# Down-projection of a decoder layer: one weight sum kept in DRAM, other bank order, other order of the last rows

## The reference

```python
D_MODEL = 2048; SEQ = 512; D_FF = 5632; EPS = 1e-6

def rms_norm(x, g):
    return x * lax.rsqrt(jnp.mean(x * x, axis=-1, keepdims=True) + EPS) * g

def conv_glu_ffn(h, w_up, conv_w, conv_b, w_down):
    u = h @ w_up
    c = causal_depthwise_conv_width_3(u, conv_w) + conv_b
    gate, val = jnp.split(c, 2, axis=-1)
    return (jax.nn.gelu(gate, approximate=True) * val) @ w_down   # (512, 5632) @ (5632, 2048)

x = x + rms_norm(y, g_mix_post)            # attention part, unchanged here
f = conv_glu_ffn(rms_norm(x, g_ffn_pre), w_up, conv_w, conv_b, w_down)
x = x + rms_norm(f, g_ffn_post)
```

## Time and profile before

| | us |
|---|---|
| time before, median of 3 runs | 2064.43 (2063.61 to 2065.13) |
| the profiled execution, its own time | 2064.49 |
| its span, from the first to the last instruction | 2062.7 |
| PE busy | 1998.8 (97%) |
| DVE busy | 1545.6 (75%) |
| ACT busy | 1012.3 (49%) |
| mean granted TensorE clock | 0.993 of full speed |

### The profile page before, as it was taken

One profiled execution on the slowest core, in us unless ns is written; L12 is line 12 of the kernel. 1 busy time (PEld: TensorE's weight loads), 2 busy tenths in 40 slices (PEclk: granted clock), 3 DMA queues, 4 the chain that ended last, 5 costly groups with the idle time before them and its releaser, 6 DMA issues.

```text
span 2062.7 us, 31761 instructions
## 1 busy us (share of the span) xinstructions
PE 1998.8 (97%) x12510; PEld 1796.4 (87%) x12510; DVE 1545.6 (75%) x2028; ACT 1012.3 (49%) x1549; POOL 0.7 (0%) x6
## 2 busy tenths in 40 slices
PE   8999999999999889999999999999999999999994
PEld 6888888888887789999999999999999787878773
DVE  5522543445446889898898889888998998899998
ACT  7422433435435655555555555545555554554442
POOL 0000000000000000000000000000000000000000
PEclk9999999999999999999999999999999999999998
DMA  8433232211636534324423432442344776668793
GB/s 317 138 123 118 77 93 82 82 62 62 244 124 211 177 103 160 119 100 151 149 101 121 163 117 100 136 163 101 111 145 154 237 245 211 224 214 295 254 361 125
DMA packets 218895, 323.26 MB, mean 157 GB/s; under 512 B 9134, under 2 KB 140622, under 8 KB 216444
## 3 DMA queue, kind: packets, MB, share of 16 engines
q1 hardware_dynamic: 218076, 315.99, 45.0%
q10 hardware_dynamic: 672, 5.24, 0.6%
HBM read 292.60 MB, written 32.54 MB: 158 GB/s over the span
## 4 chain that ended last, share of the span: by engine, by line
PE 83%; DVE 10%; issue 3%; ACT 3%; DMA 1%; DVEq 0%; SPq 0%; ACTq 0%
PE ring L2034 11%; PE ring L2036 11%; PE ring L2035 11%; PE ring L2295 9%; PE ring L2297 9%; PE ring L2296 9%; PE side L2295 4%; PE side L2297 4%; PE side L2296 4%; PE side L2034 2%; PE side L2035 2%; PE side L2036 2%; DVE w_lo L1721 2%; DVE raw L1730 1%; PE side L2110 1%
## 5 line engine op out<-in xcount | busy, mean ns | idle before, releaser
L1442 DVE TENSOR_TENSOR w_lo<-raw,w_hi 128x512 fp32r<-128x512 f32 x256 | 169.7, 688 | 275.2 <-ACT w_hi L1027 275.2
L1721 DVE TENSOR_TENSOR w_lo<-q,w_hi 128x1024 fp32r<-128x1024 f32 (+1 forms) x262 | 308.3, 1177 | 79.7 <-ACT w_hi L1244 69.5
L2295 PE MATMUL ring<-s_hi,w_hi 128*128 128x256 f32 x1008 | 286.8, 284 | 6.7 <-ACT snaps L1336 3.5
L2296 PE MATMUL ring<-s_lo,w_hi 128*128 128x256 f32 x1008 | 286.4, 284 | 0.0
L2297 PE MATMUL ring<-s_hi,w_lo 128*128 128x256 f32 x1008 | 286.4, 284 | 0.0
L1721 DVE TENSOR_TENSOR w_lo<-raw,w_hi 128x1024 fp32r<-128x1024 f32 x214 | 249.3, 1173 | 37.1 <-ACT w_hi L1244 26.9
L1027 ACT ACTIVATE w_hi<-raw 128x512 fp32r<-128x512 f32 x256 | 151.8, 624 | 187.7 <-PE ring L2036 171.1
L1244 ACT ACTIVATE w_hi<-q 128x1024 fp32r<-128x1024 f32 x174 | 183.6, 1056 | 97.5 <-PE side L2297 54.2
L2295 PEld LDWEIGHTS ring<-s_hi,w_hi 128*128 128x128 f32 x1008 | 194.8, 193 | 7.3 <-ACT snaps L1336 3.9
L2295 PE MATMUL ring<-a_hi,w_hi 128*128 128x256 f32 x688 | 195.3, 284 | 4.0 <-issue 3.3
L2034 PE MATMUL ring<-w_hi,act_hi 128*128 128x512 f32 x488 | 192.9, 395 | 3.3 <-DVE w_lo L1442 2.7
(11 more groups left out here) (298 smaller groups left out, 4672.8 us busy)
## 6 DMA issues: line engine op xcount, KB each, us to landing
q<-in_w_up SPq DMA_DIRECT2D x65, 1024.0 KB, 5.0
q<-in_w_down SPq DMA_DIRECT2D x66, 512.0 KB, 4.5
raw<-in_w_down SPq DMA_DIRECT2D x66, 512.0 KB, 4.5
raw<-in_w_in SPq DMA_DIRECT2D x28, 1024.0 KB, 5.4
raw<-in_w_out SPq DMA_DIRECT2D x24, 1024.0 KB, 4.9
raw<-in_w_up SPq DMA_DIRECT2D x23, 1024.0 KB, 6.9
q<-sa_d SPq DMA_DIRECT2D x22, 512.0 KB, 4.4
raw<-in_w_mem_kv SPq DMA_DIRECT2D x8, 1024.0 KB, 7.1
```

The costliest lines, as they stand in the source:

```text
L1442: dve.tensor_tensor(w_lo[:, s, q], raw[:, s, q], w_hi[:, s, q].bitcast(F32), ALU.subtract).then_inc(lo_done, 1)
L1721: dve.tensor_tensor(lo, src, hi.bitcast(F32), ALU.subtract).then_inc(hp_lo_done, 1)
L2295: pe.matmul(dst, hi, b_hi, start=first, stop=False, skip_group_check=True)
L2296: pe.matmul(dst, hi, b_lo, start=False, stop=False, skip_group_check=True)
```

## The change

- T3 is stored to DRAM in passes 0 and 1 (`spill_t3`, 44 stores of 256 KB to the new `t3_d`), each issued by SP one `w` after the DVE sum it stores. Passes 2 and 3 load it back in place of one weight block and make T2 from it with one addition; T1 is not made there. A step of these passes is loaded by three DMAs of 256 KB instead of two of 512 KB. The first four loads of pass 2 wait for stores that have just been issued.
- In passes 0 and 1 T3 and T1 are made by one 1024-column addition with a repeated operand instead of two of 512 columns.
- The products get other halves and banks (half 0: p3 in `bank_x`, p7 in `bank_y`; half 1: p1 in `bank_v`, p5 in `bank_w`). ACT copies three products per m out of PSUM instead of one (`keep` of "12", "21", "11"), and only p5's bank is freed by a DVE sum.
- At the end the order is half 0 for m = 0 and 1, then half 1 for m = 0 and 1; the rows are finished in the order 0, 1, 2, 3. The mean of the n = 0 half is prepared earlier on DVE (`mean0`) and added inside ACT's square root. The n = 0 half of rows 0 and 1 is finished by PE and ACT: two fp32 matmuls for each 512 columns (diagonal of rstd times f, identity times x1), then an ACT copy (`row_diagonal`, `row_out`).

```diff
-TAIL_T = (0, 2, 1, 3)
+TAIL_T = (0, 1, 2, 3)
@@ load_down(d), spill_t3(d), in the loop of SP
                 if v < 2:
-                    both(0, k1)
-                    sp.dma_start(seg(d, 2), w_down_d[k2, n2]).then_inc(down_in[s], 16)
+                    sp.dma_start(seg(d, 2, 2)..., w_down_d[k1, :]...[:, :, n1]).then_inc(down_in[s], 16)
+                    sp.dma_start(seg(d, 0), w_down_d[k2, n2]).then_inc(down_in[s], 16)
                 else:
-                    both(2, k1)
-                    both(0, k2)
+                    k = p if v == 2 else 2 * N_PAIRS - 1 - p
+                    sp.wait_ge(t3_out[k % 4], 16 * (k // 4 + 1))
+                    if 2 * N_PAIRS <= d < 2 * N_PAIRS + 4:
+                        sp.wait_ge(t3_out[s], 16 * ((d - 4) // 4 + 1))
+                    sp.dma_start(seg(d, 1), t3_d[v % 2, p]).then_inc(down_in[s], 16)
+                    sp.dma_start(seg(d, 3), w_down_d[k1, n1]).then_inc(down_in[s], 16)
+                    sp.dma_start(seg(d, 0), w_down_d[k2, n1]).then_inc(down_in[s], 16)
+            def spill_t3(d):
+                v, p = pass_pair(d)
+                sp.wait_ge(block_sum, block_sum_count(d, "T3"))
+                sp.dma_start(t3_d[v, p], seg(d, 1)).then_inc(t3_out[d % 4], 16)
...
                     sp.wait_ge(hp_lo_done, H_DOWN + e - 6)
                     load_down(e // 2)
+                e = w - H_DOWN + 4
+                if e >= 0 and e % 2 == 0 and e < 4 * N_PAIRS:
+                    spill_t3(e // 2)
...
-            for i, t in enumerate(TAIL_T):
-                for n in range(2):
-                    sp.wait_ge(out_ready, 2 * i + n + 1)
+            for n, t in ((1, 0), (1, 1), (0, 0), (1, 2), (0, 1), (0, 2), (1, 3), (0, 3)):
+                if n or t > 1:
+                    sp.wait_ge(out_ready, t + 1 if t < 2 else 2 * t - n)
+                else:
+                    sp.wait_ge(row_kept, 2 * t + 2)
@@ ACT
                 if w in (w_at(0), w_at(1)):
+                    for what in ("12", "21"):
+                        for m in range(2):
+                            keep(w == w_at(1), what, m)
+                if w in (w_at(0) + 1, w_at(1) + 1):
                     for m in range(2):
-                        keep(w == w_at(1), m)
+                        keep(w == w_at(1) + 1, "11", m)
...
+            f_square(1, 0)
+            row_root(0)
+            f_square(1, 1)
+            row_root(1)
+            row_diagonal(0)
+            row_diagonal(1)
+            for t in range(2, TT):
                 f_square(1, t)
-                take_root(NB_F + i, 1)
+                row_root(t)
+            row_out(0)
+            row_out(1)
@@ DVE
             def sums_a(d):
-                plus(d, 3, 1, 2)
-                dve.wait_ge(block_sum, block_sum_count(d, "T3"))
-                plus(d, 1, 1, 0)
+                if d >= 4:
+                    dve.wait_ge(t3_out[d % 4], 16 * (d // 4))
+                halves = raw_slots[d % 4].rearrange("p (b h n) -> p b h n", b=2, h=2)
+                b12 = seg(d, 3)
+                dve.tensor_tensor(halves[:, :, 1, :], halves[:, :, 0, :], both_times(b12), ALU.add)...
             def sums_b(d):
-                plus(d, 3, 3, 2)
-                dve.wait_ge(block_sum, block_sum_count(d, "T1"))
                 plus(d, 1, 1, 3)
...
-                if w == w_at(0) or w == w_at(1):
-                    sum_f(w == w_at(1), "12a", 0)
-                    sum_f(w == w_at(1), "12a", 1)
                 if w == w_at(0) + 1 or w == w_at(1) + 1:
-                    for m in range(2):
-                        sum_f(n, "22a", m)
-                        sum_f(n, "21a", m)
                     sum_f(n, "12b", 0)
                     sum_f(n, "12b", 1)
+                    for m in range(2):
+                        sum_f(n, "21a", m)
+                        sum_f(n, "22a", m)
+                    sum_f(n, "12c", 0)
+                    sum_f(n, "12c", 1)
...
+            for m in range(2):
+                dve.wait_ge(down_ready, m + 1)
+                for what in ("11", "12", "22", "21b"):
+                    sum_f(1, what, m)
+                times_gain(TT + m, 1, m)
+                if m == 1:
+                    for k in range(2):
+                        dve.wait_ge(down_ready, 3 + k)
+                        sum_f(1, "21", k)
+                finish(m, (1,))
+            for t in (2, 3):
+                times_gain(TT + t, 1, t)
+                finish(t)
@@ PE
-            for m in range(2):
-                for half, names in ((0, ("p6", "p2")), (1, ("p4",))):
+            for half, names in ((0, ("p6", "p2")), (1, ("p4",))):
+                for m in range(2):
...
+            pe.wait_ge(x1_back, 16 * TT)
+            for t in range(2):
+                pe.wait_ge(diag_ready, t + 1)
+                for h in range(2):
...
+                    pe.matmul(row_bank(t)[h][:, :], diagonal(t), f0[:, t, h, :], start=True, stop=False)
+                    pe.matmul(row_bank(t)[h][:, :], ident[:, :], x1_back_at[:, t, ...],
+                              start=False, stop=True).then_inc(row_added, 1)
```

More of the change, by code:

```diff
@@ L531, in build @@
         down_in = [sem(f"down_in{i}") for i in range(4)]
+        t3_out = [sem(f"t3_out{i}") for i in range(4)]
+        mean_ready, diag_ready, row_added, row_kept = (sem("mean_ready"), sem("diag_ready"), sem("row_added"),
+                                                       sem("row_kept"))
         x1_back, g_f_in = sem("x1_back"), sem("g_f_in")
@@ L670, in blocks_in @@
         def blocks_in(d):
-            return down_in[d % 4], sum(32 if True else 0 for k in range(d % 4, d + 1, 4))
+            return down_in[d % 4], sum(32 if k < 2 * N_PAIRS else 48 for k in range(d % 4, d + 1, 4))
         def block_sum_count(d, name):
             if d < 2 * N_PAIRS:
-                return 2 * d + ("T3", "T1").index(name) + 1
-            return 4 * N_PAIRS + 3 * (d - 2 * N_PAIRS) + ("T1", "T2", "T4").index(name) + 1
+                return d + 1
+            return 2 * N_PAIRS + 2 * (d - 2 * N_PAIRS) + ("T2", "T4").index(name) + 1
         def half_width(e):
@@ L740, in f_row, with diagonal, row_bank @@
             return (f0, f1)[n][:, t, :, :]
+        def diagonal(t):
+            return tokens[:, 3072 + t * P:3072 + (t + 1) * P]
+        def row_bank(t):
+            return (bank_x, bank_y)[t % 2]
         def w_at(v):
@@ L1266, in item_to_hi, with keep @@
                 act.activation(left_at(kind, slot)[0], stage_at(i), ACT.Copy).then_inc(a_hi_done, 1)
[L1268 removed]
+            def keep(n, what, m):
                 act.wait_ge(a_lo_done, (N_A0_ITEMS, N_F1_ITEMS)[n])
[L1271 removed]
+                bank = {"12": bank_x, "21": bank_y, "11": bank_v}[what]
+                act.activation(f_at(n, m, what), bank[m][:, :], ACT.Copy).then_inc(f_kept, 1)
             def f_square(n, t):
@@ L1421, in _, with row_root, row_diagonal, row_out @@
                 half_to_hi(e)
-            for i, t in enumerate(TAIL_T):
+            def row_root(t):
+                act.wait_ge(mean_ready, t + 1)
+                act.wait_ge(f_squared, TT + t + 1)
+                act.activation(root[:, NB_F + t, 0:1], ssq_f[:, t, 1:2], ACT.Sqrt, bias=mean0[:, t:t + 1],
+                               scale=1.0 / D).then_inc(root_ready, 1)
+            def row_diagonal(t):
+                if t == 0:
+                    act.wait_ge(a_lo_done, len(ITEMS))
+                act.wait_ge(rstd_ready, NB_F + t + 1)
+                act.activation(diagonal(t), ident[:, :], ACT.Copy, scale=rstd[:, NB_F + t, 0:1]).then_inc(diag_ready, 1)
+            def row_out(t):
+                for h in range(2):
+                    act.wait_ge(row_added, 2 * t + h + 1)
+                    act.activation(f0[:, t, h, :], row_bank(t)[h][:, :], ACT.Copy).then_inc(row_kept, 1)
+            f_square(1, 0)
[5 more added lines that the diff above has]
+            for t in range(2, TT):
                 f_square(1, t)
-                take_root(NB_F + i, 1)
+                row_root(t)
+            row_out(0)
+            row_out(1)
         @block.vector
@@ L2384, in _ @@
             for d in range(N_STEP - 4):
-                for half, names in enumerate((("p1", "p5"), ("p7", "p3")) if d < 2 * N_PAIRS else (("p6", "p2"), ("p4",))):
+                for half, names in enumerate((("p3", "p7"), ("p1", "p5")) if d < 2 * N_PAIRS else (("p6", "p2"), ("p4",))):
                     operands(d, half)
@@ L2398, in _ @@
                     mm.then_inc(down_ready, 1)
+            pe.wait_ge(x1_back, 16 * TT)
+            for t in range(2):
+                pe.wait_ge(diag_ready, t + 1)
+                for h in range(2):
+                    if t == 0:
+                        pe.wait_ge(f_summed, sum_count(0, "21", h))
+                        pe.wait_ge(f_gained, TT)
+                    else:
+                        pe.wait_ge(f_summed, sum_count(1, "11", h))
```

(3 more changed lines are left out.)

118 lines of the change are left out of this document (56 added, 62 removed).

## The result

Before 2064.78 us (median of 4 runs: the three of the table above and one more), after 2046.96 (2046.55 to 2047.82, 4 runs): ratio 0.9912, 95% interval 0.9900 to 0.9924. The forecast was 2049.1 with a range of 2044.5 to 2057. The profiled executions have spans of 2062.7 and 2044.8, 17.9 less where 15.3 were forecast. Each trace is of one execution, and that of the changed kernel was the fastest of its four (2046.55), so differences of a few tenths between traces of different kernels are readings, not effects shown.

What follows compares the result with a forecast made beforehand. TensorE bounds mid-pass, waits for VectorE sums at pass ends, and VectorE bounds the end. Gains 1.5 + 0.8 + 3.2 + 1.8 + 2.9 + 5.1 = 15.3 us off 2064.4 give 2049.1, range 2044.5 to 2057.

Steps and rivals of the forecast that it cites:

- Start: 1591 to 1655 us: VectorE gains 0.15 us in each of 11 steps, shortening TensorE's waits; gain 1.5 us (0 to 2.1).
- Pass 3, pass ends: 1950 to 2000 us: gain 0.8; shorter TensorE waits at the three pass ends: 0.7, 1.4 and 0.8, together 2.9 us.
- only the end pays: Rival: repeated operand costs what it saves, ScalarE copies keep pass-end waits; gain 10.9 us, time 2053.5, chance 0.15.
- 2000 to 2019: Stretch in those microseconds: the VectorE step falls from 4.90 to 4.36 us, TensorE doesn't wait; gain 3.2 us (1 to 3.2).
- Last four steps: Steps 84 to 87, to the first sweep's end: VectorE's low halves come earlier; gain 1.8 us (1 to 2.8).
- Let T be the end of step 83, now 2019.1: Time origin for the four steps after it: the sweep ends at T+13.5 now, T+11.7 after the change.
- Last rows: From the first sweep's end E to VectorE's end: E+26.5 becomes E+21.4 with the new row order; gain 5.1 us.
- That is 2 us inside DVE's end, so it costs nothing.: End of kernel: row 1's TensorE-made half, its ScalarE copy and store finish 2 us inside VectorE's end; price nothing.
- DMA and SP price nothing: 44 T3 stores of 256 KB in passes 0 and 1, and SP's waits at steps 44 to 47, stay hidden; cost nothing.
- The low clock: Rival, last sweep: TensorE falls to 1.2 GHz after idling; up to +10.9 us, time 2050 to 2060, chance 0.12.

Runs made afterwards that it cites:

- two_adds: The changed kernel with two 512-column additions instead of the merged 1024-column one in passes 0 and 1; 2048.94 us, ratio 0.9918.
- banks_only: The kernel before with the new banks, ScalarE copies and merged addition, without the T3 store and with the old last rows; 2062.05 us, ratio 0.9982.
- act_drains: The changed kernel with ScalarE also copying the fourth pair of banks and pass-end sums spread over four half steps; 2044.95 us, ratio 0.9903.
- store_only: The kernel before with T3 stored to DRAM and loaded back, old banks and old last rows; 2055.11 us, ratio 0.9950.
- no_store: The changed kernel without the T3 store: passes 2 and 3 load four blocks and use three additions a step; 2059.83 us, ratio 0.9970.
- full_loads: The changed kernel loading 1024 KB a step again in passes 2 and 3, one block unused; 2048.59 us, ratio 0.9919.
- store_less: The changed kernel without one of its eight last stores, row 0's first half, which is not written; 2047.79 us, ratio 0.9915.
- both_better: The changed kernel with ScalarE draining the fourth pair of banks and row 1 finished before the sums of rows 2 and 3; 2044.75 us, ratio 0.9902.

## Why the prediction was right, and where it was off

The time was 2 us below the forecast. In the main the mechanism was the one given: VectorE relieved and the banks drained earlier where TensorE waits, and shorter last rows. The sum was helped by luck: two misses, 3.0 and 1.6 us, have opposite signs, and the start came out near its forecast for another reason than the one given.

**Start.** Right in size (1.9 for 1.5, the bound being 2.1), wrong in cause. The term was VectorE's 0.15 us in each of 11 steps. two_adds shows that this is worth 0.3; the other 1.6 come with the new order of the products, which the prediction gave nothing at the start. Why the order frees TensorE there was not taken apart.

**Pass 3, pass ends.** Right. The merged addition took 1.220 us where the subtraction as its stand-in took 1.226, and waits at the pass ends are gone, so "only the end pays" is out; banks_only, 4.3 less with the old end, says the same. The wait at 1 to 2 came as forecast, a `lo` behind eight sums:

```profile
1725.10 0.50 PE L2099 MATMUL side<-w_hi,act_lo 128*128 128x512 f32 x1 [1.08 <-DVE f L1957]
...
1850.85 0.50 PE L2099 MATMUL side<-w_hi,d_tok 128*128 128x512 f32 x1 [0.99 <-DVE w_lo L1780]
```

Lost 1.3 us there where I had 1.4. act_drains bears out that it is the sums: the wait goes when ScalarE drains the fourth pair and the sums are spread (the two were not tried apart). At 2 to 3 it is the missing addition, as said: TensorE loses 2.2 us there in store_only and in the changed kernel, 3.4 in banks_only and 3.2 before.

**2000 to 2019.** Right: up to the end of step 83, now at 2008.2, no wait of TensorE is left.

**Last four steps.** This step failed in size: 1.8 forecast, 4.8 measured. "Let T be the end of step 83, now 2019.1" was misread. The six matmuls before 2019.1 are step 84's, and the wait at 2022.45 is that of step 85: step 83 ended at 2017.2, so T to E was 15.4, not 13.5 (and the 3.2 of the term above took in step 84). The kernel before:

```profile
2017.56 0.50 PE L2034 MATMUL side<-w_hi,d_res 128*128 128x512 f32 x1 [0.17 <-DVE w_lo L1721]
...
2026.79 0.50 PE L2034 MATMUL side<-late,d_tok 128*128 128x512 f32 x1 [1.41 <-DVE late L1721]
```

The four low halves that TensorE takes up at 2017.56, 2022.45, 2026.79 and 2031.13 are those of steps 84 to 87. Against that the new sweep stands as computed but for VectorE being 1.1 us less late:

```profile
2010.09 0.50 PE L2099 MATMUL side<-w_hi,d_tok 128*128 128x512 f32 x1 [0.35 <-DVE w_lo L1780]
...
2013.70 0.51 PE L2099 MATMUL side<-late,d_tok 128*128 128x512 f32 x1 [1.95 <-DVE late L1780]
...
2017.32 0.50 PE L2099 MATMUL side<-late,d_snap 128*128 128x512 f32 x1 [1.96 <-DVE late L1780]
```

T = 2008.2, the last wait ends at T+9.1 for my T+10.2, E = T+10.6. 1.9 + 1.1 is the whole miss; why VectorE was 1.1 less late than computed stays open. no_store confirms the place: 6.1 us of what the store is worth lie in these steps.

**Last rows.** 5.7 for 5.1: VectorE ended at E+20.9 for E+21.4. The schedule held, ScalarE's diagonal of row 1 at 2030.68 included (it held the square of row 2, and VectorE 0.19 us).

**"That is 2 us inside DVE's end, so it costs nothing."** This step is wrong by 1.6 us. Row 1's store was issued 2.3 us before VectorE's end, as said. I counted the issues that stand behind it (0.6 each) and not the bytes: four stores of 512 KB take 5.2 us of all DMA engines. Before, the stores went in pairs seven microseconds apart and the last landed 3.1 after its issue.

**DMA and SP price nothing.** Right. Landing times rose in pass 0 (medians of 4.7 to 5.8 us for 256 KB, for the 4.5 of the earlier trace rows) and TensorE didn't see it. SP's four waits of steps 44 to 47 came, 14.2 us in all where I had some 5 each, and the loads behind them had landed by 1840.2, ten microseconds before TensorE began pass 2:

```profile
SPq L920 <- DMA t_d<-raw: 7.8, 2, 4.0
SPq L920 <- DMA t_d<-q: 6.4, 2, 3.5
```

full_loads shows that the traffic of passes 2 and 3 doesn't matter either. The batching rule of the Trainium skill (DMA: Bandwidth & Descriptors, Measured) did not bind here: three transfers of 256 KB a 4.1 us step flowed, 230 GB/s in all, those of weights landing in 3.6 us and those of T3 in 2.9, against 4.9 for 512 KB before, in the same 70 us of pass 2:

```profile
q<-in_w_down SPq DMA_DIRECT2D x19, 256.0 KB, 3.6
...
q<-t_d SPq DMA_DIRECT2D x9, 256.0 KB, 2.9
```

**The low clock.** It did not come in the changed kernel's profiled sweep (1.00 from 2017.5 to 2029). Ten traces have its waits (two of some 1.95 us idle in the last steps), and it came in three of them: two_adds and store_less lost 2.0 to 2.1 us to it, and both_better ran five matmuls at 0.43 us inside a wait it had anyway. In the four traces without the store the first wait is 3.2 to 3.3 us, and all four have matmuls at 1.2 GHz after it. So the rival was real at its small size, never at its 10.9. What I took from the Trainium skill (TensorE: Matmul & The Clock Gate, What's actually happening), that idle PE falls to 1.2 GHz, agrees with these traces in direction; but starts 2.35 us apart were followed by either clock, so the length of one gap doesn't tell which.

## What to carry to other kernels

An engine that is 99% busy beside the bound is worth relieving for what happens at the edges: here 30 us of VectorE's work taken out gave 9.6, half of it in the last four steps, where TensorE waited for it. A wait put into an in-order DMA queue must be priced per step, with the issues behind it, against the step: a wait of 4.2 us on average with 2.2 us of issues behind it, in a step of 5.4, uses up any lead, whatever the lead is. Behind the last compute instruction count bytes as well as instructions: here the last four outputs left at the rate of the DMA engines, so look for which of them is issued first in the last unbroken run. And when an edit of a few tenths is judged by one trace each, look at the granted clock first: two_adds met its expected number by 2 us of clock.

## What was not expected of the hardware

- Stores from SBUF to DRAM of 512 KB, one after another, run at 395 to 417 GB/s in the full slices of 0.6 to 0.7 us, before and after. Loads and stores mixed reached 395 to 415 in slices of 1.6 us (changed kernel, pass 0), so this is no gift of stores alone.
- After the same wait (starts of matmuls 2.30 to 2.36 us apart) TensorE's clock was 2.4 GHz in some executions and 1.2 in others, for some 4 us (0.50 over 2017.5 to 2022). It came back within 4.5 us there, but in no_store it stayed at 0.50 for 13 us, with an idle 1.4 us in each 4.3.
- A plain fp32 matmul of 512 columns, eight in a row, took 0.86 us each (2029.69 to 2036.55), two records of 0.43, with a granted clock of 1.00 over all of them: 0.43 between starts is there no sign of the low clock.
